# A two-block kernel: how the state-space input is scaled and turned, and the order of chunks and splits around it

## The reference, cut to what matters

```python
x = first_block(x, ...)                       # ends in a layer norm
h = rms_norm(x, mix_norm[0])                  # x / sqrt(mean(x*x) + eps) * gain
u = (h @ w_in).reshape(seq, 64, 16)           # 64 groups of 16
# for each group: a complex linear recurrence over the sequence with 64 states
bu = einsum('gnk,lgk->lgn', b, u_seq);  x_l = a * x_(l-1) + bu_l
y = real(einsum('gkn,lgn->lgk', c, x_l)) + d_skip * u
z = gelu(y);  val, gate = split(z @ w_glu, 2)
x = x + val * sigmoid(gate)
x = x + swiglu_ffn(rms_norm(x, ffn_norm[0]), ...)
ckv = rms_norm(x, kv_in_norm) @ w_kv_a        # first product of latent attention
```

## Time and profile before

| what | value |
|---|---|
| median of 3 runs | 1783.81 us (1782.95 to 1784.18) |
| the profiled execution, its own time | 1781.67 us |
| its span (first to last instruction) | 1779.7 us |
| mean granted clock of PE | 0.995 |
| PE busy | 1740.9 us, 98% of the span |
| DVE, ACT, POOL busy | 785.3, 666.3, 626.1 us |

### The profile page before, as it was taken

One profiled execution on the slowest core, in us unless ns is written; L12 is line 12 of the kernel. 1 busy time (PEld: TensorE's weight loads), 2 busy tenths in 40 slices (PEclk: granted clock), 3 DMA queues, 4 the chain that ended last, 5 costly groups with the idle time before them and its releaser, 6 DMA issues.

```text
span 1779.7 us, 22686 instructions
## 1 busy us (share of the span) xinstructions
PE 1740.9 (98%) x9006; PEld 1450.1 (81%) x9006; DVE 785.3 (44%) x1430; ACT 666.3 (37%) x1128; POOL 626.1 (35%) x299
## 2 busy tenths in 40 slices
PE   8999999999999898999999999999999999999999
PEld 6887988888788687789888888888788888888887
DVE  3877899486765557333111111148664411111111
ACT  3433344243233755433222312266654333122221
POOL 4433203304204322424443434343801245344342
PEclk9999999999999899999999999999999999999999
DMA  9422244443545457223333233232101233333332
GB/s 241 96 80 84 69 135 139 144 131 116 156 122 166 138 199 243 84 70 115 95 95 95 89 101 98 77 91 77 48 1 36 73 107 95 95 95 95 100 96 77
DMA packets 242279, 189.60 MB, mean 107 GB/s; under 512 B 41472, under 2 KB 199296, under 8 KB 242176
## 3 DMA queue, kind: packets, MB, share of 16 engines
q1 hardware_dynamic: 240304, 182.80, 34.6%
q10 hardware_dynamic: 1872, 5.37, 0.9%
HBM read 168.74 MB, written 19.40 MB: 106 GB/s over the span
## 4 chain that ended last, share of the span: by engine, by line
PE 89%; DVE 5%; ACT 3%; issue 1%; DMA 1%; POOL 1%; DVEq 0%; SPq 0%; ACTq 0%
PE ps L377 14%; PE ps L379 14%; PE ps L378 14%; PE ps L403 10%; PE ps L404 10%; PE ps L405 10%; PE ps L434 3%; PE ps L436 3%; PE ps L435 3%; PE ps L880 2%; PE ps L861 2%; PE ps L871 1%; PE ps L658 1%; DVE x_rows L1686 1%; PE ps L853 1%
## 5 line engine op out<-in xcount | busy, mean ns | idle before, releaser
L1021 POOL TENSOR_TENSOR w_lo<-w_raw,w_hi 128x1024 fp32r<-128x1024 f32 (+4 forms) x251 | 589.8, 2360 | 1092.6 <-ACT w_hi L1170 1092.6
L377 PE MATMUL ps<-a_hi,w_hi 128*128 128x512 f32 (+1 forms) x1184 | 442.2, 373 | 0.0
L379 PE MATMUL ps<-a_hi,w_lo 128*128 128x512 f32 (+1 forms) x1184 | 440.5, 372 | 0.0
L378 PE MATMUL ps<-a_lo,w_hi 128*128 128x512 f32 (+1 forms) x1184 | 440.3, 372 | 0.0
L1170 ACT ACTIVATE w_hi<-w_raw 128x1024 fp32r<-128x1024 f32 (+3 forms) x283 | 283.1, 1019 | 210.6 <-DMA w_raw<-in_ffn_w_gate_up_dram 70.9
L377 PEld LDWEIGHTS ps<-a_hi,w_hi 128*128 128x128 f32 x1184 | 223.1, 188 | 40.3 <-issue 1.9
L379 PEld LDWEIGHTS ps<-a_hi,w_lo 128*128 128x128 f32 x1184 | 223.0, 188 | 38.8
L378 PEld LDWEIGHTS ps<-a_lo,w_hi 128*128 128x128 f32 x1184 | 223.1, 188 | 38.3
L2163 DVE TENSOR_TENSOR ev<-ps,xh 128x512 f32<-128x512 f32 x44 | 30.4, 692 | 411.9 <-PE ps L379 382.9
L403 PE MATMUL ps<-w_hi,h_hi 128*128 128x512 f32 x476 | 188.6, 396 | 2.0 <-DVE x_rows L1656 1.5
L405 PE MATMUL ps<-w_hi,h_lo 128*128 128x512 f32 x476 | 187.8, 395 | 0.0
(11 more groups left out here) (347 smaller groups left out, 2346.5 us busy)
## 6 DMA issues: line engine op xcount, KB each, us to landing
w_raw<-in_ffn_w_gate_up_dram SPq DMA_DIRECT2D x88, 512.0 KB, 3.8
w_raw<-in_w_up_dram SPq DMA_DIRECT2D x44, 512.0 KB, 4.0
w_raw<-in_ffn_w_down_dram SPq DMA_DIRECT2D x40, 512.0 KB, 3.7
w_raw<-in_w_in_dram SPq DMA_DIRECT2D x20, 512.0 KB, 4.4
w_raw<-in_w_down_dram SPq DMA_DIRECT2D x20, 512.0 KB, 3.8
s_records<-stage SPq DMA_DIRECT2D x16, 544.0 KB, 5.3
w_raw<-in_ssm_w_glu_dram SPq DMA_DIRECT2D x16, 512.0 KB, 3.8
rec<-s_records SPq DMA_DIRECT2D x14, 544.0 KB, 5.4
```

The costliest lines, as they stand in the source:

```text
L377: pe.matmul(bank, wh, xh_, start=first, stop=False)
L378: pe.matmul(bank, wh, xl_, start=False, stop=False)
L379: return pe.matmul(bank, wl, xh_, start=False, stop=last)
L1021: pool.tensor_tensor(w_lo[:, n % RING, 0:w], w_raw[:, n % RING, 0:w], w_hi[:, n % RING, 0:w].bitcast(F), ALU.subtract).then_inc(lo_made, 1)
```

## The change

1. PE turns `x_rows` itself and no longer a scaled copy (`tile_turner` with `ln_ready` in place of `xh_turner`); ACT's scaled copy L1365 goes. The inverse deviations (`st[:, 8:12]`, one per row) go to a DRAM tensor of 512 numbers and come back in the order of the product's rows, as `rms_by_step`, by one store and two loads on SP; `even_rows` and `odd_rows` multiply by them.
2. On ACT the squares, roots and splits of stage `mix0` are written out in a new order. On DVE `split_tile(1)` moves ahead of `ln_rows(3)`, `rms(2)` behind it, and `rms(3)` to the end.
3. In the scan, ACT makes the chunk of `made_in` at the end of the round and not at its start; POOL makes more decays ahead of each of those chunks' low parts; DVE splits the turned-back output at the start of its round and not after `add_swapped`.
4. In stage `mla` ACT makes the third `kv_a` chunk after the split of tile 0, ahead of the square of tile 2.

```diff
--- before.py
+++ after.py
@@ -91,6 +91,7 @@
             mla_q_nope_norm_2, mla_q_rope_norm_2, mla_w_o_2,
             c_ident, c_rope, c_decay, c_count, c_freq, c_mask, out):
     rec_dram = nc.dram_tensor("s5_records", [NB, P, REC], F, kind="Internal").ap()
+    rms_dram = nc.dram_tensor("s5_rms", [SEQ], F, kind="Internal").ap()
     with ExitStack() as ctx:
         ctx.enter_context(nc.allow_non_contiguous_dma(reason="small parameter tables"))
         base = (nc.sbuf_base + 31) // 32 * 32
@@ -121,6 +122,7 @@
         ps_c = fixed("ps_c", [P, POOLG], F)
         st = fixed("st", [P, 192], F)
         eps_c = fixed("eps_c", [P, 4], F)
+        rms_by_step = st[:, 136:140]
         arena = (at_now[0] + 511) // 512 * 512
         room = nc.sbuf_top - arena
 
@@ -249,6 +251,8 @@
         gate_pre = sem("gate_pre")
         gate_conv = sem("gate_conv")
         gate_act = sem("gate_act")
+        rms_out = sem("rms_out")
+        rms_in = sem("rms_in")
         u_even = sem("u_even")
         sv_turned = sem("sv_turned")
         sv_swapped = sem("sv_swapped")
@@ -684,7 +688,8 @@
 
             def mix0_first():
 
-                mix0.extend(xh_turner("mix0"))
+                mix0.extend(tile_turner("mix0", lambda t, k: x_rows[:, t, k * P:k * P + P],
+                                        lambda t: pe.wait_ge(ln_ready, t + 1)))
 
                 def after(t, n):
                     if t == 0 and n == 2:
@@ -1008,7 +1013,7 @@
                 pool.tensor_copy(r8_c[:, b_ % 2, :, 1:], d).then_inc(decay_made, 1)
 
             first_gate = chunks_at[("u", 1, 0)] + TT
-            decays_from = {0: range(0, 6), 1: range(6, 7), 2: range(7, 11), 3: range(11, 13), 4: range(13, NB)}
+            decays_from = {0: range(0, 6), 1: range(6, 9), 2: range(9, 13), 3: range(13, 15), 4: range(15, NB)}
             for n, (_, kn, cn, _) in enumerate(chunk_src):
                 if n in vector_chunks:
                     continue
@@ -1119,6 +1124,13 @@
                 for f in range(NB):
                     if chunks_at[("s5k", f)] + RING + 1 == n:
                         store_batch(f)
+                if n == chunks_at[("u", 1, 0)] + 1:
+                    sp.wait_ge(rms_made, TT)
+                    sp.dma_start(rms_dram.rearrange("(t p) -> p t", p=P), st[:, 8:12]).then_inc(rms_out, 16)
+                    sp.wait_ge(rms_out, 16)
+                    for i in range(2):
+                        sp.dma_start(rms_by_step[NC * i:NC * i + NC, :],
+                                     rms_dram.rearrange("(c j a) -> a c j", a=2, j=T // 2)[i]).then_inc(rms_in, 16)
                 if n == chunks_at[("u", 1, 0)] + 3:
                     stores_landed()
                     for b_ in range(2, RECS):
@@ -1205,10 +1217,12 @@
                 for k in range(2):
                     split((stage, t, k), *dst(t, k))
 
-            def rms_and_split(stage, added, ready, dst):
+            def rms_and_split(stage, added, ready, dst, chunks=0):
 
                 deviation(stage, added, ready, 0)
                 for t in range(TT):
+                    if t == 1:
+                        make(chunks)
                     if t + 1 < TT:
                         deviation(stage, added, ready, t + 1)
                     split_tile(stage, t, dst)
@@ -1353,21 +1367,27 @@
             down = lambda t: ("f1", "down", 2, 1, t)
 
 
-            whole = lambda t: (ln_ready, t + 1)
+            def square_sums(t):
+
+                act.wait_ge(ln_ready, t + 1)
+                step(act.activation(xh[:, t % 2, :], x_rows[:, t, :], ACT.Square, accum_out=st[:, t:t + 1]))
+                act.activation(st[:, 4 + t:5 + t], st[:, t:t + 1], ACT.Sqrt, scale=1.0 / D,
+                               bias=eps_c[:, 1:2]).then_inc(sq_ready, 1)
+
             ln_deviation(down, 1, 0)
             limit[0] += 1
             make(limit[0])
-            for t in range(TT):
-                deviation("mix0", down, whole, t)
-                if t + 1 < TT:
-                    ln_deviation(down, 1, t + 1)
-                act.wait_ge(rms_made, t + 1)
-                act.activation(xh[:, t % 2, :], x_rows[:, t, :], ACT.Copy, scale=st[:, 8 + t:9 + t])\
-                   .then_inc(xh_ready, 1)
-                if t and t < TT - 1:
-                    split_tile("mix0", t - 1, to_a_s5)
-            split_tile("mix0", TT - 2, to_a_s5)
-            split_tile("mix0", TT - 1, to_a_s5)
+            ln_deviation(down, 1, 1)
+            square_sums(0)
+            ln_deviation(down, 1, 2)
+            square_sums(1)
+            split_tile("mix0", 0, to_a_s5)
+            square_sums(2)
+            split_tile("mix0", 1, to_a_s5)
+            ln_deviation(down, 1, 3)
+            split_tile("mix0", 2, to_a_s5)
+            split_tile("mix0", 3, to_a_s5)
+            square_sums(3)
             limit[0] = 10 ** 6
             make(chunks_at[("u", 0, 0)] + 1)
             for i in range(2):
@@ -1381,8 +1401,10 @@
             def odd_rows(half, j):
                 b = at(("u", half, j))
                 act.wait_ge(u_even, 4 * half + j + 1)
+                act.wait_ge(rms_in, 32)
                 release(("u", half, j), act.activation(u_c[:, 32 * half:32 * half + 32, 2 * j + 1, :],
-                                                       b[NC:P, :].rearrange("c (g k) -> c g k", k=GK), ACT.Copy))
+                                                       b[NC:P, :].rearrange("c (g k) -> c g k", k=GK), ACT.Copy,
+                                                       scale=rms_by_step[NC:P, j:j + 1]))
 
             for j in range(4):
                 odd_rows(0, j)
@@ -1420,9 +1442,6 @@
             make(limit[0])
             s5_turned(0)
             for b_ in range(NB):
-                if b_ in made_in:
-                    limit[0] = first_gate + made_in[b_]
-                    make(limit[0])
                 if b_ in rows_in:
                     odd_rows(1, rows_in[b_])
                 if b_ + 1 < NB:
@@ -1433,6 +1452,9 @@
                 if b_ in back_in:
                     split(("zt", back_in[b_]), *turned_back(back_in[b_]))
                 swap_scanned(b_)
+                if b_ in made_in:
+                    limit[0] = first_gate + made_in[b_]
+                    make(limit[0])
             s5_gelu(NB - 2)
             split(("zt", KT - 2), *turned_back(KT - 2))
             s5_gelu(NB - 1)
@@ -1453,7 +1475,7 @@
 
 
             added = lambda t: ("f2", "down", 2, 1, t)
-            rms_and_split("mla", added, bank_ready(added), to_a)
+            rms_and_split("mla", added, bank_ready(added), to_a, chunks_at[("kv_a", 0)] + 3)
 
             for t in range(TT):
                 ahead(chunks_at[("kv_a", t)])
@@ -2067,19 +2089,20 @@
             split_tile("mix0", 0, to_a_s5)
             add(3)
             ln_stats(3)
+            split_tile("mix0", 1, to_a_s5)
+            ln_rows(3, 1, ln_ready)
             rms(2)
-            ln_rows(3, 1, ln_ready)
-            split_tile("mix0", 1, to_a_s5)
-            rms(3)
             split_tile("mix0", 2, to_a_s5)
             split_tile("mix0", 3, to_a_s5)
+            rms(3)
             go(v.memset(zc[:, :, :, 0:1], 0.0))
             go(v.memset(zs[:, :, 0:1], 0.0))
             settle()
             def even_rows(half, j):
-                v.tensor_copy(u_c[:, 32 * half:32 * half + 32, 2 * j, :],
-                              full(v, ("u", half, j))[0:NC, :].rearrange("c (g k) -> c g k", k=GK))\
-                 .then_inc(u_even, 1)
+                v.wait_ge(rms_in, 32)
+                v.tensor_scalar(u_c[:, 32 * half:32 * half + 32, 2 * j, :],
+                                full(v, ("u", half, j))[0:NC, :].rearrange("c (g k) -> c g k", k=GK),
+                                rms_by_step[0:NC, j:j + 1], None, ALU.mult).then_inc(u_even, 1)
 
             for j in range(4):
                 even_rows(0, j)
@@ -2094,6 +2117,8 @@
             for b_ in range(NB):
                 if b_ in rows_in:
                     even_rows(1, rows_in[b_])
+                if b_ - 1 in back_in:
+                    split(("zt", back_in[b_ - 1]), *turned_back(back_in[b_ - 1]))
                 r = b_ % RECS
                 b = full(v, ("sv", b_))
                 v.wait_ge(rec_state[r], 32 * (b_ // RECS + 1))
@@ -2102,8 +2127,6 @@
                 w = release(("sv", b_), v.tensor_tensor(z1[:, :], b[:, 0:256], cs, ALU.mult))
                 if b_:
                     add_swapped(b_ - 1)
-                if b_ - 1 in back_in:
-                    split(("zt", back_in[b_ - 1]), *turned_back(back_in[b_ - 1]))
                 v.wait_ge(*w)
                 v.wait_ge(sv_swapped, 2 * (b_ + 1))
                 step(v.tensor_tensor(z1[:, :], z1[:, :], sv_sw[:, :], ALU.subtract))
```

## The result

The changed kernel takes 1788.11 us in the median of 7 runs (1787.63 to 1790.61), the kernel before 1783.11 in 7 beside them (1781.69 to 1784.18): +5.0 us, ratio 1.0033, 95% interval 1.0023 to 1.0043. It is slower, by 0.3%. It grows along the kernel.

A forecast was written before the change was run, and what follows sets the result against it. PE, busy 98% of the span, was taken as the bound. Terms 0.45 - 0.3 + 0.85 + 1.0 + 1.65 + 1.5 = 5.15, rounded to +5.0 on 1783.81, gave 1788.8 us; own range 1786.8 to 1790.8, 8 in 10 1783.2 to 1791.2.

The forecast's parts named there:

- Input's turning: State-space input: two added DVE stalls of 1.5 us and an earlier split make tile 3 ready at 604.05, +0.45 us.
- Round trip hidden: Store and two loads of the inverse deviations end at 620.5, before the first move at 625.69; cost 0.
- Moves at nothing: The product's moves from PSUM now multiply, 0.64 us against 0.68 as a copy; costed at nothing.
- The scan's loop: Scan rounds 6 to 15: chunk rounds 6.50 us instead of 6.80, rounds with a split 4.58; -0.3 us.
- Part 2's sum: Scan changes (change 3): -0.3 for the loop, +0.85 for batch 14's output, +1.0 for the clock: +1.55 us.
- Output of batch 14: Scan's end: the add releasing PE's output of batch 14 stands behind the 1.09 us split, +0.85 us.
- Clock at the tail: After PE idles about 2.6 us before batch 14's output, the granted clock falls: +1.0 us (0 to 1.7).
- The latent chunk: Latent input: ACT blocks on the third chunk's landing, PE waits 3.6 us, loses 1.98: +1.65; clock fall +1.5 (0 to 2.5).
- the clock did not hold: Rival: both gaps, scan's end and latent input, leave the clock at 2.4 GHz; 1786.3 us, chance 0.18.
- the latent chunk blocked: Rival: the third latent chunk lands before 1165.7 and doesn't block, up to 1.98 us gained; 1783.7 us, chance 0.08.
- POOL's low part did disturb: Rival: POOL's low part disturbs nobody in its new scan round, three rounds give 3.3 us back; 1785.5 us, chance 0.08.
- the small transfers: Rival: the deviations' transfers come late, over 8.5 us a leg; at 10 a leg +3, 1791.8 us, chance 0.05.

The follow-up runs named there:

- e1: Part 1 alone (changes 1 and 2: input rows turned unscaled, new order of stage mix0) on the kernel before: 1783.21 us, +0.7.
- e5: Changes 1 and 2 on the kernel before, with the reciprocals of the deviations moved behind the normed rows on DVE: 1780.56 us, -2.3.
- e7: Change 3 on the kernel before, with the first of the four chunks left at its old place ahead of round 4's odd rows: 1783.15 us, +0.3.
- e2: Change 3 alone (the scan's decays, chunks and turned-back splits) on the kernel before: 1784.32 us, +1.9.
- e11: Whole change on the kernel before, with reciprocals behind normed rows, first scan chunk in its old place, third latent chunk one tile later: 1779.05 us, -3.3.
- e3: Change 4 alone (third latent chunk made after the split of tile 0) on the kernel before: 1784.45 us, +2.0.
- e12: As e7, with POOL's low-part subtraction for the other three chunks replaced by a fill with zeros: 1778.13 us, -4.2 against the kernel before.
- e9: e4 and e5 together on the kernel before, without change 3: 1776.24 us, -6.1.
- e4: Change 4 alone on the kernel before, with the third latent chunk made one tile later: 1778.01 us, -4.5.

## Why the prediction was right, and where a term was off

The forecast was 1788.8, the result 1788.1, the ratio's interval +4.1 to +7.7 us. By steps:

- **Input's turning, +0.45.** Tile 3 was turned 0.24 late in the profile and 0.43 in e1. Both added stalls are there, at 1.73 where I had 1.5. e5 shows that these stalls and the early split kept tile 3 back by 3.5 us (600.52 against 604.03 in e1; 3.4 by my sum). Part 1 alone: +0.7, interval around zero. I gave this place no clock term; the changed kernel and e1 show a longer low stretch there, 1.5 us, and the profiled e7, which has nothing of part 1, shows it too (first move at 627.26 after a turning at 603.66, clock 0.50 to 612). So it is luck of an execution at least in part, and what part 1 adds to it stays open.
- **Round trip hidden.** Right, but with 2.5 us to spare and not 5: the store was mis-sized, 10.1 us for 6.1, and the loads took 6.8.
- **Moves at nothing.** 0.74 on DVE for 0.68.
- **The scan's loop, -0.3.** Chunk rounds 6.41 to 6.48 (6.5 forecast), split rounds 4.51 to 4.72 (4.58). The loop by itself gained 0.4 (e7). Missing was one step, of the kind that I had promised to follow: I counted what stands behind a moved `make` for three of the four chunks. Behind the first, on ScalarE, stand the odd rows of round 4, and they free the bank that PE needs for its turning 5: +1.0. Part 2's sum by that is +2.55; e2 measured +1.9.
- **Output of batch 14, +0.85.** In the changed kernel the offset grows by 0.75 between DVE's round 15 (719.28, against 716.75) and this output, and PE idles 2.29 (2.6 forecast).
- **Clock at the tail, +1.0.** From that output to the first product of the second half (737.05 against 732.32) the offset grows from 3.28 to 4.73: 1.45. Low slices before and after the gap, above. The size was right for this execution, but a gap of this length doesn't fix it: behind 2.29, 2.31 and 2.44 us the clock fell (the changed kernel, e2, e11), behind 2.42 in e7 it did not.
- **The latent chunk, +1.65 and clock +1.5.** PE waits 3.45 (3.6 forecast), the wait of 1.98 is gone, the clock falls. In the two profiles the stage costs 2.9 (3.15 forecast), but +2.0 in the medians of e3. The size that was off is the fall: I charged it wholly to the change, and by the profiles above the kernel before likely pays the same 1.5 in many executions behind its 1.98. The one profiled execution that I had showed none. Nor did my upper bound of 2.5 hold for each execution: e3's profile lost 2.0 more in this stage than the changed kernel's.

The forecast's two misses, the bank (+1.0) and the clock that before likely also pays (between 0 and -1.5), nearly cancelled. That the forecast came within 0.7 us of the result is luck to that extent; the mechanisms that it named are all in the rows. The rivals: the clock did not hold; the latent chunk blocked; POOL's low part did disturb, and e12 gives its price, 1.0 a round, 2.9 in all, near the 3.3 of the rival's working; the small transfers were 4.4 us late (about 624.9 against 620.5) without reaching the path. That rival's own threshold was a little low: (625.69 - 608.3) / 2 is 8.7 us a leg, so 10 a leg would have cost 2.6 and not 3.

On the halved clock as the default, which activity releases (the Trainium skill, TensorE: Matmul & The Clock Gate, "What's actually happening"): behind a wait of 3.45 the trace agrees, with 0.50 at 1176 to 1178. Behind one of 1.98 at the same place the kernel before stayed at 1.00 and e1 showed 0.57 in the mean of 1176 to 1180, so a single profile doesn't tell what such a gap costs. On VectorE with two SBUF inputs and GpSimd reading SBUF, which lock each other out for a whole instruction (the Trainium skill, SBUF — State Buffer, "SBUF: two separate sides"): 1.44 us with the subtraction of GpSimd beside it and 0.42 without agree with it.

## What to carry to other kernels

When work is moved ahead on an in-order engine, list everything that it now stands in front of, for every instance of it and not for the typical one: a copy that only frees a bank, or a square that only a far engine needs, can be what PE waits for next. Making a chunk sooner pays only after its transfer has landed; one tile later turned +2.0 us into -4.5. An early result that nobody needs soon (the reciprocals) should stand behind the work that feeds the bound engine, even when it is 0.16 us long, for its wait is not. And a clock fall seen, or not seen, in one profile is one draw: look at the same stage in every other kernel's profile, and at the mean granted clock of each execution, before charging it to a change.

## What the runs showed of the hardware

- A store of 512 single numbers out of SBUF held SP 10.1 us (608.03 to 618.13) in the changed kernel and 9.5 us in e9 (603.59 to 613.13), while the small loads of the earlier trace rows took 6.1.
- After the input's turning each profiled execution shows between none (e12) and three (e2, the changed kernel) stretches at the half clock from 640 to 760 us, some of them in slices where PE is busy throughout (4.00 of 4.00 at 0.64, above). Where they fall differs between executions of nearly equal schedules (684 in the kernel before, 678 and 708 in e4, which only differs far behind). The cause was not separated.
- The same wait of PE is followed by the half clock in some executions and not in others: 1.98 us in front of the third latent chunk in five profiles of eight, 1.73 to 1.74 us for `prob` in seven of fourteen, 2.3 to 2.4 us before the output of batch 14 in three of four. The first costs the stretch behind it 1.5 us (42.47 without, 43.97 to 44.05 with the fall).
- The time of an execution goes with its mean granted clock: the kernel before took 1779.9 to 1780.1 us at 0.996 and 1781.3 to 1784.1 at 0.992 or 0.993.
- VectorE's subtraction of two SBUF tiles took 1.44 us beside GpSimd's subtraction and 0.42 without it (e12), 1.0 us a round.
